# A decoder step on one core: the query projection in three products of rounded parts, and the large phase's operands made at the stage's end

## The reference

```
x  = x + mix @ w_out
h  = rms_norm(x, norm2_g)
q  = rms_norm((h @ w_query) as 8 heads x 256, qnorm_g)      # the query projection, 1024 x 2048
s1 = q[..., :128] @ subkeys[:, 0].T ; s2 = q[..., 128:] @ subkeys[:, 1].T    # 128 keys each
top 16 of s1, top 16 of s2, top 16 of their 256 sums -> 16 experts a head, gates g by softmax
a  = gelu(h . u[e]) ;  x = x + sum_e g a v[e]               # 16384 experts
```

## Time and profile before

| | us |
|---|---|
| median of 3 runs (lowest, highest) | 1492.38 (1489.86, 1492.73) |
| the profiled execution | 1489.78 |
| its span | 1488.0 |
| PE busy | 1471.1 (99%) |
| DVE busy | 1144.4 (77%) |
| ACT busy | 594.5 (40%) |
| POOL busy | 450.9 (30%) |
| the fp32 products of 260 columns with `hT` as the moving operand (L1790, 768 passes), busy | 169.9 |
| the two groups of the up projection (L2129), busy | 417.4 and 409.5 |

### The profile page before, as it was taken

The page is one execution under the profiler, slowest core; times in us unless marked ns, Lnnn a source line. Parts: engine busy times, 40 slices in busy tenths (PEclk is TensorE's granted clock), DMA queues, the critical chain, the costliest instruction groups (busy, mean ns, idle before and its releaser), DMA issues.

```text
span 1488.0 us, 24983 instructions
## 1 busy us (share of the span) xinstructions
PE 1471.1 (99%) x9696; PEld 1281.1 (86%) x9696; DVE 1144.4 (77%) x2499; ACT 594.5 (40%) x984; POOL 450.9 (30%) x433
## 2 busy tenths in 40 slices
PE   9999999999999999999999999999999999999999
PEld 7834444788888999999999999999999899999998
DVE  8729885676799899856777777525379799999995
ACT  2003125510223533454555555535344344444442
POOL 0000214412056576510000000000277567766530
PEclk9999999999999999999999999999999999999999
DMA  5243373402321155655888888887799999999992
GB/s 206 76 109 140 106 276 115 172 1 89 122 99 65 58 171 177 231 194 187 274 279 284 284 282 275 273 290 261 286 412 405 408 413 417 414 416 411 409 397 93
DMA packets 143237, 356.21 MB, mean 239 GB/s; under 512 B 26696, under 2 KB 100832, under 8 KB 128528
## 3 DMA queue, kind: packets, MB, share of 16 engines
q1 hardware_dynamic: 127232, 310.04, 57.4%
q0 software_dynamic: 15600, 44.50, 8.3%
q10 hardware_dynamic: 288, 0.07, 0.0%
HBM read 283.23 MB, written 71.25 MB: 238 GB/s over the span
## 4 chain that ended last, share of the span: by engine, by line
PE 86%; DVE 9%; DMA 3%; ACT 1%; issue 1%; SPq 0%; DVEq 0%; ACTq 0%
PE psum L2129 31%; PE psum L2181 27%; PE psum L1790 21%; PE psum L2150 4%; DMA v_raw<-in_v 1%; DMA qrow<-d_q 1%; PE psum L1932 1%; PE psum L2011 1%; DVE u_a L1549 1%; PE psum L1796 0%; DVE kprod L1216 0%; PE psum L1950 0%; DVE sSc L1217 0%; PE psum L1849 0%; PE psum L1901 0%
## 5 line engine op out<-in xcount | busy, mean ns | idle before, releaser
L2129 PE MATMUL psum<-h_h,u_g 128*128 128x260 f32 x2048 | 417.4, 285 | 2.7 <-DVE u_a L1549 2.6
L2129 PE MATMUL psum<-h_y,u_a 128*128 128x260 f32 x2048 | 409.5, 282 | 0.0
L2181 PE MATMUL psum<-w_h,v_g 128*128 128x448 f32 x1024 | 376.0, 367 | 0.9 <-DVE w_y L1728 0.9
L2181 PE MATMUL psum<-w_y,v_a 128*128 128x448 f32 x1024 | 373.8, 365 | 0.0
L2129 PEld LDWEIGHTS psum<-h_h,u_g 128*128 128x128 f32 x2048 | 314.1, 188 | 3.5 <-DVE u_a L1549 2.8
L2129 PEld LDWEIGHTS psum<-h_y,u_a 128*128 128x128 f32 x2048 | 315.3, 188 | 0.0
L1549 DVE TENSOR_TENSOR u_a<-u_raw,u_g 128x1024 fp32r<-128x1024 f32 x128 | 151.3, 1226 | 141.0 <-ACT u_g L980 140.9
L792 POOL DMA_INDIRECT t_dots<-d_acts,t_lists x72 | 112.4, 1562 | 426.6 <-DMA d_acts<-act_f 404.9
L2181 PEld LDWEIGHTS psum<-w_h,v_g 128*128 128x128 f32 x1024 | 192.2, 188 | 18.5 <-DVE v_a L1722 1.3
L2181 PEld LDWEIGHTS psum<-w_y,v_a 128*128 128x128 f32 x1024 | 192.3, 188 | 15.3
L1722 DVE TENSOR_TENSOR v_a<-v_raw,v_g 128x1024 fp32r<-128x1024 f32 x128 | 156.5, 1223 | 50.9 <-ACT v_g L1010 50.7
(11 more groups left out here) (399 smaller groups left out, 1716.5 us busy)
## 6 DMA issues: line engine op xcount, KB each, us to landing
u_raw<-in_uT SPq DMA_DIRECT2D x64, 1024.0 KB, 7.5
v_raw<-in_v SPq DMA_DIRECT2D x32, 2048.0 KB, 15.2
d_act<-act_f SPq DMA_DIRECT2D x32, 896.0 KB, 10.8
d_gate<-stage SPq DMA_DIRECT2D x14, 2048.0 KB, 12.0
a_in<-d_act SPq DMA_DIRECT2D x32, 896.0 KB, 7.3
g_in<-d_gate SPq DMA_DIRECT2D x32, 896.0 KB, 10.1
wr<-in_w SPq DMA_DIRECT2D x13, 2048.0 KB, 8.2
kv<-in_ck SPq DMA_DIRECT2D x24, 256.0 KB, 8.3
```

What stands on the lines that cost most here:

```text
L2129: mm = pe.matmul(upair[n % 2][:, cols], w, hs[:, k, cols], start=(k == 0 and x == 0), stop=(k == KT - 1 and x == 1))
L2181: mm = pe.matmul(ybank[m][:, 0:DENSE], w, z[g % 2][:, c, :], start=(q == 0 and x == 0), stop=(last and x == 1))
```

## The change

The query projection no longer takes `hT`. The gained activations are split into `h2_high` (rounded to fp32r by ScalarE's copy) and `h2_low` (what is left, by VectorE's `hidden_rest`). Each chunk of the weights is split too: `wq_high`, a ring of three, by ScalarE (`query_weights_rounded`), and `wr_low`, in the place of the weights, by a subtraction on GpSimd (`query_weights_rest`). TensorE adds high x high, high x low and low x high, three fp32r products in place of one fp32 product. GpSimd makes the first three subtractions before the loop and one ahead of each of the units 0 to 12.

`h_h` and `h_y` are no longer made ahead of the loop. VectorE normalises `xT` in place, a slice in each of the turns 7 to 14 (`hidden_grown`), ScalarE makes `h_h` among the score copies of head 6 (`hidden_rounded`), and VectorE makes all of `h_y` in turn 17 (`hidden_left`). `U_LOW_AT` starts at turn 15 instead of 17, one more group is made by turns, and the `AT_` constants grow by three or four.

```diff
-AT_EXP = 31
-AT_TABLES = 34
-AT_GATES = 45
-AT_FIRST = 109
-AT_PREPARE = 115
+AT_EXP = 34
+AT_TABLES = 37
+AT_GATES = 49
+AT_FIRST = 113
+AT_PREPARE = 119
...
-U_LOW_AT = {17: [(0, 0), (0, 1)], 18: [(0, 2), (0, 3)], 19: [(1, 0), (1, 1)], 20: [(1, 2), (1, 3)],
-            23: [(2, 0), (2, 1)], 24: [(2, 2), (2, 3)]}
-U_LOW_AT.update({25 + 2 * j: [(3 + j, x) for x in range(4)] for j in range(5)})
-FIRST_LOOPED = 11
+U_LOW_AT = {15: [(0, 0), (0, 1)], 16: [(0, 2), (0, 3)], 18: [(1, 0), (1, 1)], 19: [(1, 2), (1, 3)],
+            21: [(2, 0), (2, 1)], 22: [(2, 2), (2, 3)]}
+U_LOW_AT.update({23 + 2 * j: [(3 + j, x) for x in range(4)] for j in range(6)})
+GROWN_AT, LEFT_AT = 7, 17
+QUERY_CHUNKS = 2 * H
+QRING = 3
+FIRST_LOOPED = 12
...  GpSimd
+            def query_weights_rest(j):
+                cols = slice(j % 4 * P, (j % 4 + 1) * P)
+                b = WGROUPS.index(f"wq{j // 4}") % 2
+                pool.wait_ge(wq_rounded, j + 1)
+                pool.tensor_tensor(wr_low[b][:, :, cols], wr[b][:, :, cols], wq_high[j % QRING][:, :, :].bitcast(F32),
+                                   ALU.subtract).then_inc(wq_rest, 1)
+
+            for j in range(QRING):
+                query_weights_rest(j)
...
             for u, (h, i, r) in enumerate(UNITS):
+                if u + QRING < QUERY_CHUNKS:
+                    query_weights_rest(u + QRING)
...  ScalarE
+            def query_weights_rounded(j):
+                w = weights_arrived(act, f"wq{j // 4}")
+                if j >= QRING:
+                    arrived(act, ("wq", j - QRING, 1))
+                A(wq_high[j % QRING][:, :, :], w[:, :, j % 4 * P:(j % 4 + 1) * P], ACT.Copy).then_inc(wq_rounded, 1)
+
+            def hidden_rounded(ks):
+                arrived(act, ("wq", QUERY_CHUNKS - 1, 1))
+                for k in ks:
+                    act.wait_ge(hn_done, k + 1)
+                    A(h_h[:, k, :], xT[:, k, :], ACT.Copy, scale=1.0 / GROW).then_inc(hhi_done, 1)
...
+            for m in range(KT):
+                for f in range(2):
+                    emptied(act, ("wo", m, f))
+                if m == KT - 1:
+                    for j in range(QRING):
+                        query_weights_rounded(j)
+                A(h2_high[:, m, :], xT[:, m, :], ACT.Copy, scale=par[:, P_G2 + m:P_G2 + m + 1]).then_inc(h2_rounded, 1)
...
             def queries(h, a):
+                if QRING <= 2 * h + a + 2 < QUERY_CHUNKS:
+                    query_weights_rounded(2 * h + a + 2)
...  VectorE
+            def hidden_rest(m):
+                v.wait_ge(h2_rounded, m + 1)
+                stt(h2_low[:, m, :], xT[:, m, :], par[:, P_G2 + m:P_G2 + m + 1], h2_high[:, m, :].bitcast(F32),
+                    ALU.mult, ALU.subtract).then_inc(h2_done, 1)
...
-                ts(hT[:, m, :], xT[:, m, :], par[:, P_G2 + m:P_G2 + m + 1], None, ALU.mult).then_inc(h2_done, 1)
                 do(tt(sq2T[:, m, :], xT[:, m, :], xT[:, m, :], ALU.mult), sq2_done)
+                if m >= 1:
+                    hidden_rest(m - 1)
+            hidden_rest(KT - 1)
...
+            def hidden_grown(k):
+                if k == 0:
+                    v.wait_ge(x_parked, 16)
+                stt(xT[:, k, :], xT[:, k, :], par[:, P_G2 + k:P_G2 + k + 1], rstd2[:, :], ALU.mult, ALU.mult
+                    ).then_inc(hn_done, 1)
+
+            def hidden_left(k):
+                v.wait_ge(hhi_done, k + 1)
+                stt(h_y[:, k, :], h_h[:, k, :].bitcast(F32), 1.0 - GROW, xT[:, k, :], ALU.mult, ALU.add).then_inc(hs_done, 1)
...
+                if 0 <= u - GROWN_AT < KT:
+                    hidden_grown(u - GROWN_AT)
+                if u == LEFT_AT:
+                    for k in range(KT):
+                        hidden_left(k)
                 for g, s in U_LOW_AT.get(u, []):
                     u_rest(g, s)
...  TensorE
             def query(h, a):
                 m = 2 * h + a
-                w = weights_arrived(pe, f"wq{m // 4}")
+                low = wr_low[WGROUPS.index(f"wq{m // 4}") % 2]
+                cols = slice(m % 4 * P, (m % 4 + 1) * P)
+                pe.wait_ge(wq_rounded, m + 1)
                 for f in range(2):
                     bk = claim(pe, ("wq", m, f))
-                    product(bk[:, 0:HALF], [(w[:, k, (m % 4) * P:(m % 4 + 1) * P], hT[:, k, halves[f]])
-                                            for k in range(KT)], ("wq", m, f), h2_done)
+                    for k in range(KT):
+                        if m == 0 and f == 0:
+                            pe.wait_ge(h2_done, k + 1)
+                        for n, hs in enumerate((h2_high, h2_low)):
+                            pe.matmul(bk[:, 0:HALF], wq_high[m % QRING][:, k, :], hs[:, k, halves[f]],
+                                      start=(k == 0 and n == 0), stop=False)
+                    if f == 0:
+                        pe.wait_ge(wq_rest, m + 1)
+                    for k in range(KT):
+                        mm = pe.matmul(bk[:, 0:HALF], low[:, k, cols], h2_high[:, k, halves[f]],
+                                       start=False, stop=(k == KT - 1))
+                    made(mm, ("wq", m, f))
```

More of the change, by code:

```diff
@@ L212, in trunk_and_peer @@
     since, until = rates[:, 0:LATER], rates[:, LATER:LATER + SEQ]
+    h2_low = put("h2_low", [P, KT, NT], F32R, hs0)
     c0 = hs0 + HT
@@ L276, in trunk_and_peer @@
     qT = put("qT", [P, NPT, 4, P], F32, E0)
+    h2_high = put("h2_high", [P, KT, NT], F32R, B0)
     mixA = put("mixA", [P, 4, NT], F32, B0)
@@ L313, in trunk_and_peer @@
     wr = [put(f"wr{b}", [P, KT, 512], F32, W0 + 16384 * b) for b in range(2)]
+    wr_low = [put(f"wr_low{b}", [P, KT, 512], F32R, W0 + 16384 * b) for b in range(2)]
+    wq_high = [put(f"wq_high{b}", [P, KT, P], F32R, at) for b, at in enumerate((c0, c0 + 4096, k0 + 8256))]
     X0 = W0 + 32768
@@ L431, in trunk_and_peer @@
     ms_ready, ms_exp, ms_made, ms_out, Cp_out = sems("ms_ready ms_exp ms_made ms_out Cp_out")
-    sq2_done, h2_done, hn_done, hhi_done, hs_done, ms_rows = sems(
-        "sq2_done h2_done hn_done hhi_done hs_done mean_square_rows")
+    sq2_done, h2_done, hn_done, hhi_done, hs_done, ms_rows, h2_rounded, wq_rounded, wq_rest = sems(
+        "sq2_done h2_done hn_done hhi_done hs_done mean_square_rows h2_rounded wq_rounded wq_rest")
     g_sub, g_exp, tb_done, tb_high = sems("g_sub g_exp tb_done tb_high")
@@ L1032, in _ @@
                     if (g, a) == (H - 2, 1):
-                        act.wait_ge(hs_done, KT)
+                        act.wait_ge(hn_done, 1)
                         for s in range(4):
@@ L1041, in _ @@
                     scores_out(h * NPT + i)
+                    if h == H - 2:
+                        hidden_rounded((2 * i, 2 * i + 1))
             act.wait_ge(head_squares, 1)
@@ L1414, in _ @@
                     continue
-                if m == 0:
-                    arrived(v, ("mM", NTT - 1))
-                ts(hT[:, m, :], xT[:, m, :], par[:, P_G2 + m:P_G2 + m + 1], None, ALU.mult).then_inc(h2_done, 1)
                 do(tt(sq2T[:, m, :], xT[:, m, :], xT[:, m, :], ALU.mult), sq2_done)
+                if m >= 1:
+                    hidden_rest(m - 1)
+            hidden_rest(KT - 1)
             for f in range(2):
@@ L1618, in _ @@
             for s in range(4):
-                u_rest(8, s)
+                u_rest(9, s)
             for i in range(NTT):
@@ L1636, in _ @@
             for s in range(4):
-                u_rest(9, s)
+                u_rest(10, s)
             n64 = DB * H
@@ L1676, in _ @@
             for s in range(4):
-                u_rest(10, s)
+                u_rest(11, s)
             for i in range(NPT):
```

## The result

| | before | after |
|---|---|---|
| device time, median (range) | 1491.12 us (1489.31 to 1492.73, 4 runs) | 1510.95 us (1508.86 to 1513.19, 4 runs) |
| ratio to before, 95% interval | | 1.0134 [1.0113, 1.0154] |
| span of the profiled execution | 1488.0 us | 1511.0 us (device time 1513.19) |
| first `up` product | 513.02 us | 532.05 us |
| first `down` product | 1062.81 us | 1082.85 us |

A forecast was written before the change was run, and what follows sets the result against it. VectorE's top-k loop was taken as the bound; its terms put `u_rest(2, 2)` 17.5 us later, so the profiled 1489.78 us becomes 1507.3, and 2.6 for the median gives 1509.9, say 1510. Range given: 1481 to 1519.

The forecast's parts named there:

- The bound: VectorE's top-k loop sets the kernel's end through `u_rest(2, 2)`, done at 566.1 instead of 548.57, 17.5 us later; TensorE waits.
- The price of the subtraction: One GpSimd subtraction of 128x1024 takes 2.35 us (ends 1.84 and 2.53); thirteen are issued in the loop.
- Where it lands: The subtraction runs 1.35 to 3.70 us into VectorE's turn and holds `abf` 2.19 us in twelve turns: 26.3 us.
- The start: VectorE's loop starts at 396.6 instead of 404.20: 12.96 us less work, mean square 3.0 later, fourth subtraction 2.35.
- The third term: Ahead of the mean square, VectorE's last `hidden_rest` takes 0.7 us and ends at 380.3.
- Turn 4: VectorE's loop waits for head 1's scores, there at 417.7 where VectorE would be at 416.1: 1.6 us.
- `hidden_grown`: Eight slices in VectorE's turns 7 to 14 add 0.69 us each, 5.5 us, and 0.2 each for a fold in progress.
- The end of the loop: Before `up`, group 0's `u_rest` adds 4.7 us and `hidden_left` 5.5; `up` starts at 531.9, 18.9 us later.
- Moved counts and what follows: From 566 on, tables, gates and first down loads moved by three or four counts cost nothing, bounds -1 and +3.
- only two operands: Rival: in VectorE's loop only two-operand operations are held, 1.25 us a turn, 15.0 in place of 26.3: 1499, chance 0.12.
- GpSimd's pace: Rival: GpSimd sets the loop's pace altogether, each turn 0.5 us longer or more: 1518 to 1523, chance 0.05.
- slow products: Rival: query products run at 0.221 us each, 10.6 us a chunk, making the kernel 55 us slower; chance 0.01.

The follow-up runs named there:

- e1: Changed kernel without the thirteen GpSimd subtractions in the loop, the high part of the weights multiplied a second time instead: 1483.35 us, 0.9939 of the kernel before.
- e2: Changed kernel with four GpSimd writes of zeros in place of each of the thirteen subtractions in the loop: 1487.16 us, 0.9960 of the kernel before.
- e7: Changed kernel with GpSimd's subtraction moved behind its wait for `eq`, and `hidden_grown` moved to just ahead of `eq`: 1494.93 us, 1.0019 of the kernel before.
- e8: Changed kernel with 130 extra products on TensorE ahead of its wait for `h_y`: 1514.25 us, 1.0142 of the kernel before.
- e4: Changed kernel with the fp32 query projection of before, keeping the later operands and moved counts: 1489.28 us, 0.9971 of the kernel before.
- e9: e7 with the large phase's operands made two turns earlier and one more group inside the selection: 1478.81 us, 0.9917 of the kernel before.
- e5: Changed kernel with each of GpSimd's thirteen subtractions in the loop made twice in a row: 1533.89 us, 1.0272 of the kernel before.

## Why the prediction was right

The forecast of 1510 stands against 1510.95, and its mechanism was the one that e1, e2 and e7 show. The two times are closer than the two changes: I forecast 17.5 us on top of 1492.38, and measured are 19.8 us on top of 1491.12, which the kernel before took in this comparison. Step by step:

- **The bound.** `u_rest(2, 2)` was to be done at 566.1; it was at about 565.9 (the pair of subtractions starts at 564.69 and takes 2.34). But the step that TensorE would wait for it failed: it came later, at 567.8, by its lowered clock, a term that the sum did not have. e8 takes that away, and the wait is there.
- **The price of the subtraction.** 2.35 us forecast, 2.37 to 2.46 measured in the loop (the three ahead of it take 7.99 together).
- **Where it lands.** 1.35 us into the turn forecast; 434.81 - 433.40 = 1.41. `abf` was held for 2.1 us in turns 3, 5, 6 and 7, and `abu` for 2.0 in turns 8 to 14. I had twelve turns; it was eleven (turn 3 and 5 to 14): the subtraction of turn 4 (418.39) fell into a wait of VectorE's for scores.
- **The start.** 3.0 us later mean square forecast, 4.3 measured (386.56 against 382.22). The third term, VectorE's `hidden_rest`, was itself held, the same effect that I had used for the loop and the inverse root but not here: beside GpSimd's sums it took 1.88 or 1.89 us instead of 0.7, and the last one, on which TensorE waits 0.9 us, took 1.77 beside the first subtractions. VectorE's row, then GpSimd's:

```profile
379.93 1.77 DVE L1453 SCALAR_TENSOR_TENSOR h_low<-xT,par,h_high 128x520 fp32r<-128x520 f32 x1 [1.03 <-ACT h_high L989]
...
378.31 7.99 POOL L767 TENSOR_TENSOR wr_low<-wr,wq_high 128x1024 fp32r<-128x1024 f32 x3
```

  TensorE, after 2.73 us of standing still, ran its first products at a granted clock of 0.50 (377.4 to 380.0). The fourth subtraction did hold one step of the inverse root, 2.91 us instead of 0.70, as forecast. The loop started at 397.83, 396.6 forecast.
- **Turn 4.** VectorE's wait for the scores of head 1 was forecast at 1.6 us and measured at 3.67. With one held turn fewer (2.2) and the later start, turn 5 begins at 426.03 where my terms give 425.1.
- **`hidden_grown`.** Turns of 8.24 us on average (440.74 to 506.68, eight), 8.28 forecast.
- **The end of the loop.** `hidden_left` 4.87 us (5.5 forecast), group 0 4.52 (4.7). Up starts at 532.05; 531.9 forecast. Errors of +1.2 (the start), +2.1 (turn 4), -2.2 (one held turn fewer), -0.6 (`hidden_left`) and less cancel in this: the term that carries the forecast (a price per turn times the turns) is good to some 10% (about 2.15 in eleven turns, 23.6 us, against 26.3), the closeness of the sum is luck.
- **Moved counts and what follows.** Priced at nothing, bounds -1 and +3. Up ends 20.0 us later, not 17.5. 19.2 of these stand where `u_rest(2, 2)` is used (567.8 against 548.61), 1.9 of them by the clock (567.8 - 565.9). The other 0.8 come behind it, where there are waits of 0.7 us for `act_f` and 0.6 for `u_a` that the kernel before has not; in 570 to 700 TensorE has no wait. From the first product of down to the end it is 428.15 us, 425.19 before, with 2.8 us of wait for `w_y` instead of 0.9. This is not the counts by themselves: e8 has the same counts, a wait of 1.0 us there and 425.2 us of down projection. The profiled execution took 1513.19, 5.9 over its forecast of 1507.3; it is the longest of the four runs, and their median is 2.2 below it. What the counts cost beside the clock no run separates; e4, which has them too, shows no loss by them that its interval could tell.

The rivals: "only two operands" falls by the rows of `abf` and `abu`, which have one operand and are held; "GpSimd's pace" is real but worth some 3.4 of 27.5 us (e2); "slow products" falls by the rows (eight products of the third kind end 1.12 us after the first starts).

What stays open: which of VectorE's operations are held, beyond those seen. Held were a cast, a shift with one operand, additions and products of two operands; maxima, replacements and index searches never: in the changed kernel none of those over 256 elements takes more than 0.44 us in any of the 33 turns. And whether a longer write by GpSimd would hold a cast for longer than the 0.23 us of e2.

## What to carry to other kernels

Count what an added operation on GpSimd does to VectorE by where it lands in VectorE's sequence, not by its own length or by GpSimd's idle time: 2.4 us cost 2.2 when they started 1.4 us into the turn, ahead of the cast, and 0.9 (GpSimd's own period) when they started behind `eq`, 4.0 us into it, beside searches that nothing holds (e7). If no such gap exists, the same arithmetic on the busier engine can be cheaper (1.15 us on VectorE for 2.2 us of being held). And when one engine gets faster, look at what the next phase waits for: here the saving came through only when the order of the waiting engine was set anew.

## What I had not expected of the hardware

- After 16.8 us without a product, TensorE's granted clock is 0.50 for most of its first 6 us of work, and the first 32 products take 6.67 us instead of 3.85. The same level shows behind pauses of 14.34 (e7), 7.78 (e2) and 2.73 us (the start of the stage); after 4.40 us (e1) the first products run at full speed and the level falls during the next ones (0.61 on average in 504.5 to 507). After 1.59 us (e9), and after the 2.64 us of the kernel before at 546, it stays at 1.00.
- An operation of VectorE that waits for GpSimd gets in between two subtractions issued back to back (e5), although GpSimd's next is in its queue already.
- Writes of zeros on GpSimd leave VectorE's two-operand `eq` at 0.40 us, where a subtraction stretches it to 1.77.
